# One step of a hybrid decoder layer on one core: gate rows in pieces, x squares on ScalarE, conv and value groups alternating, decode output in column groups

## The chip, the cores and the metric

The kernel runs on one core of one Trainium2 chip. Its engines work side by side, each through its own queue of instructions in order: TensorE (PE; its weight loads are shown as PEld), VectorE (DVE), ScalarE (ACT), GpSimd (POOL) and SyncE (SP, which here only issues DMAs). They wait for each other by semaphores. The metric is the time of the program on the device in microseconds; before the change it is 1457.6 us, the median of three runs (1457.57 to 1459.19).

## The reference

One inference step of a layer for 256 prompt tokens and 8 x 4 decode tokens, width 2048, float32:

```python
h = rms_norm(x, norm_mix); proj = h @ w_in          # 4360 columns: conv q/k, values, output gate, gates, q, k, v
qk = silu(causal_conv(qk_m)); h_m = mlstm_chunkwise(q_m, k_m, v_m, ig, log_sigmoid(fg), C, n, m)
h_m = rms_norm(h_m) * sigmoid(o_m)
a_out = sliding_window_attention(rms_norm(q_a), rms_norm(k_a), v_a, sinks, rel_bias)   # window 128, 16 heads, 2 kv heads
x = x + concat(h_m, a_out) @ w_out
x = x + cross_attend(rms_norm(x), mem_k, mem_v) @ wo    # 4 heads, 256 memory tokens
x = x + square(relu(rms_norm(x) @ w_up)) @ w_down       # 8192 wide
```

The outputs are x and the new states: conv rows, memory matrices C, n and m, window keys and values, memory keys and values.

## The kernel before, in words

Activations lie by feature: 128 features on the partitions, 288 tokens (256 and 32) along the row. All weights come as one stream of 388 chunks, each 512 x 256 numbers (512 KB). SP loads a chunk into one of four slots of `raw`. ScalarE rounds it to the high half `whi` (line 913), VectorE subtracts to get the low half `wlo` (line 1317), and TensorE multiplies high by high, high by low and low by high: 24 matmuls of 128x128 by 288 columns a chunk (line 457). Activations are halved alike (`a_hi`, `a_lo` for x, `b_hi`, `b_lo` for the memory and later for what goes into w_out). Four chunks make a group of 256 output columns, which ends in two of four PSUM tiles `g`; VectorE takes them out.

The first 76 chunks are one written order: groups 0 and 1 memory keys, 2 k and v, 3 to 6 queries (QA), 7 to 10 conv (QKM), 11 to 14 values (VM), 15 to 18 output gate (OM). The table `beside` says for every chunk which smaller steps each engine issues behind that chunk, and every engine goes through the same table: its own part of the chunk (ScalarE and VectorE split the chunk three ahead), then its parts of the steps, then, after a group's fourth chunk, VectorE's taking out. A step that waits on one engine therefore holds all that is queued behind it on that engine, splits and chunk matmuls too.

The steps that the change touches:
- x norm. GpSimd squares the 16 tiles of x and adds them into `nacc` (lines 1976 to 1989); `norm_x` (chunk 11) sums over the partitions with a matmul by ones, ScalarE takes the root, VectorE the reciprocal `rstd`.
- Gate rows. `gates_mm` (11) multiplies x by the gate weights; `gates_rows` (13) is one chain between VectorE and ScalarE (lines 1376 to 1437 and 968 to 978): pre-activations, Exp, Ln, two scans, two more Exp. `columns` (15) turns the rows.
- `mem_squares` (14) and `mem_norm` (18): the norm of the memory rows and keys, squares on ScalarE. `q_norm(n)` (14, 16, 17, 20, 21, 24, 25, 28, 29): square on ScalarE, matmul by a block of ones, root, reciprocal and product.
- Decode attention: `dec_scores` (30), `dec_probs` (32), `dec_out` (33). `dec_out` multiplies by 64 value columns as weights and 32 columns of probabilities as data, 32 matmuls into one bank (lines 569 to 580).
- Sliding window: eight turns of two heads, three chunks apart from chunk 33: `swa_scores` (VectorE adds the bias and takes the maximum), `swa_exp` (ScalarE, with sums), `swa_norm` (VectorE scales the probabilities), `swa_probs` (TensorE turns them, ScalarE and VectorE copy), `swa_out` one chunk on.
- `conv_taps(ct)` for the eight conv tiles at chunks 32 to 45, four multiply-adds on VectorE each; `conv_gate` for all eight at chunk 47 with Sigmoid; `v_turn`, two value tiles each at 50, 53, 56 and 60.
- Memory heads: four heads of four chunks from 60 on: `m_scores`, `m_out0`, `m_out1`, `m_state`, then `m_norm`, `m_gate`, `m_final`. In `m_norm` ScalarE loads the Sqrt table, takes the root, applies Sigmoid to the output gate, and loads Exp again.
- w_out: four turns of two column groups, each group its four chunks in the order of input tiles 8, 12, 0, 4 (`WOUT_KT`); tiles 0 to 7 come from the memory heads.
- Cross-attention (`cross`, one list for all engines) with the value chunks `mv` between, then wo, and `up`/`down` of the MLP, where `rms_total(1)` after the second chunk needs GpSimd's sum of squares.

Of the kernel before, what the change touches and what calls it, by code (L numbers as in the profile page):

```python
# [29 lines left out]
P = 128  # L30
D = 2048
# [38 lines left out]
C_END = 930  # L70
# [15 lines left out]
def constants():  # L86
# [15 lines left out]

    return c
# [26 lines left out]
def weight_stream(w):  # L130
# [7 lines left out]
    for first, groups in ((COL_QA, 4), (COL_QK, 4), (COL_V, 4), (COL_O, 4)):  # L138
        out += tiles(w["w_in"][0], every, range(first, first + groups * CW, CW))
    out += tiles(w["w_out"][0], [r * P for r in WOUT_KT], range(0, D, CW))  # L140
# [34 lines left out]
def gate_columns(w_in):  # L175
# [15 lines left out]
state_in stored memscr_out qz_zero qz_ready dz_hi dz_lo sw_exp sw_max swa_cache swa_new_out tile0_done tile_out u_hi u_lo v_T v_out  # L191
# [3 lines left out]
SLOT_SIGNALS = dict(raw_ready=4, c_in=3, c_out=3, bt_in=2, rb_in=2, vdec_in=2, mv_in=4, mem_in=4, x_in=4, mtok_in=2)  # L195
# [3 lines left out]
    pe_once=dict(xss_bc=1, gates_pre=1, gcols_T=1, kv_T=1, kv_rev=1, dsc_mm=1, dprob_T=1, dout_mm=1, km_T=1, xd_mm=1,  # L199
                 xdp_T=1, xdv_mm=2, xdo_T=1),  # L200
    act_once=dict(rstd_root=1, g_ln=1, gate_rows=1, rm_root=1, ktok_out=2, krev_out=1, kss_root=2, d_exp=1, dpw_out=1,
                  da_hi=4, km_out=2, xd_exp=1, xdp_out=2, od_act=1),
    dve_once=dict(eps_ready=1, wg_split=3, rstd_x=1, g_nz=1, g_exps=1, rm_ready=1, gcols_out=4, kdup_out=2, vtok_out=2,
                  vrev_out=1, memk_ready=8, qd_ready=4, d_max=1, dprob=1, dpn_out=1, da_lo=4, vm_ones=2, xd_max=1,
# [3 lines left out]
def layer_kernel(nc, ins, outs, consts):  # L208
    with ExitStack() as ctx:
# [78 lines left out]
        kgain = view(15328, XHD)  # L288
# [31 lines left out]
        pc, pcT = view(16000, 2, NMEM), view(16512, 2, NMEM)  # L320
# [6 lines left out]
        EPSC, TINY, SSM, RM, KSS, MX, NM, SD, ES, SM = 0, 1, 4, 6, 8, 16, 20, 24, 28, 32  # L327
        GC, WS, WM, NC_, KINV, RM2, SPARE = 36, 48, 60, 68, 104, 112, 114
# [21 lines left out]
        def _(sp):  # L350
# [16 lines left out]
            for j in range(2):  # L367
                load(memtok[:, j, :], ins["mem_prompt"][0, j * P:(j + 1) * P, :], sem["mtok_in"][j])
            with sp.Fori(2, CHUNKS // RING) as i:
# [16 lines left out]
        def dec_src(kv, par):  # L386
            return M[2][kv * HD:(kv + 1) * HD, 0:256].rearrange(
                "p (b t r l) -> p t b r l", b=DB, t=4, r=2)[:, :, :, par, :]
# [17 lines left out]

        def v_bank(i):
# [8 lines left out]
        beside[8].append(("gate_weights",))  # L416
# [14 lines left out]
        for ct in range(8):  # L431
            beside[4 * QKM + 4 + ct % 2 + 4 * (ct // 2)].append(("conv_taps", ct))
        for ct in range(8):
            beside[47].append(("conv_gate", ct))
        for g, c in enumerate((50, 53, 56, 60)):
            beside[c] += [("v_turn", 2 * g), ("v_turn", 2 * g + 1)]
        for h in range(MH):
            for c, what in ((60, "m_scores"), (61, "m_out0"), (62, "m_out1"), (63, "m_state")):
                beside[c + 4 * h].append((what, h))
            if h:  # L440
# [9 lines left out]
                 ("mv", 5), ("xo", 1), ("xs", 3), ("mv", 6), ("xp", 2), ("xm", 3), ("mv", 7), ("xo", 2), ("dv", 0),  # L450
                 ("dv", 1), ("xp", 3), ("dz",), ("xo", 3)]
# [3 lines left out]
        def _(pe):  # L455
# [28 lines left out]
            def norm_x():  # L484

                pe.wait_ge(sem["cst_in"], 16)
                pe.wait_ge(sem["sq_sum"], 16)
                mm(M[0][:, 0:NT], ones, nacc[:, :]).then_inc(sem["pe_once"], 1)
# [1698 lines left out]
```

## Time and profile before

| what | us |
|---|---|
| runs, median of three | 1457.6 |
| profiled execution, its own time | 1460.68 |
| its span, first to last instruction | 1458.9 |
| TensorE busy | 1383.3 |
| VectorE busy | 876.0 |
| ScalarE busy | 606.3 |
| GpSimd busy | 151.4 |

A row of a timeline gives the start in us from the span's start, the duration, engine, line, operation, output and inputs, shape and count; in square brackets stands the idle time of the engine before it and who ended it. "m" and "g" are the PSUM tiles of small steps and of chunks, "arena" is the working memory of most small steps.

### The profile page before, as it was taken

Reading aid. Unit: us, or ns where it says so; the run is one execution under the profiler, and the core shown is the slowest. Engines: PE = TensorE matmul, PEld = TensorE weight load, DVE = VectorE, ACT = ScalarE, POOL = GpSimd, SP = SyncE. Lnnn points to the kernel's source line nnn. Section 1 sums busy time; section 2 is a strip of 40 time slices with the busy share of each in tenths; the row PEclk is TensorE's granted clock in tenths of the full one; section 3 lists DMA queues with packets and bytes.
Section 4 is the critical chain, followed back from the end, with each engine's and each line's share of the span. In section 5 each row is a group of like instructions: output and inputs, shape, how many; then the busy total and the mean of one; then the engine's idle time right before and its main releaser. Section 6 shows DMA issues by size and latency. Waiting matters only on the chain.

```text
span 1458.9 us, 27482 instructions
## 1 busy us (share of the span) xinstructions
PE 1383.3 (95%) x10270; PEld 1349.9 (93%) x10270; DVE 876.0 (60%) x1257; ACT 606.3 (42%) x839; POOL 151.4 (10%) x199
## 2 busy tenths in 40 slices
PE   6749998899999999889999999999999999999999
PEld 6749897888889998789999999999999999999999
DVE  7767698746666667595554455544466544556543
ACT  6445355634454444453333334333343333344332
POOL 4521000011113231260000000000000000000000
PEclk9989999999899999999999999999999999999999
DMA  9754334454538568445554545555454555555553
GB/s 363 237 149 145 116 109 124 126 195 151 160 102 351 169 210 262 149 145 172 160 171 161 164 153 173 173 161 171 158 161 156 179 166 162 169 160 164 166 169 126
DMA packets 74972, 250.06 MB, mean 171 GB/s; under 512 B 8284, under 2 KB 17324, under 8 KB 74512
## 3 DMA queue, kind: packets, MB, share of 16 engines
q1 hardware_dynamic: 58176, 212.36, 44.3%
q0 software_dynamic: 16016, 36.06, 7.9%
q8 instruction: 39, 0.64, 0.2%
q10 hardware_dynamic: 720, 0.83, 0.2%
q14 instruction: 21, 0.17, 0.0%
HBM read 236.20 MB, written 13.64 MB: 171 GB/s over the span
## 4 chain that ended last, share of the span: by engine, by line
PE 80%; DVE 9%; issue 3%; ACT 3%; POOL 2%; DMA 1%; SPq 0%; DVEq 0%; ACTq 0%; POOLq 0%
PE g L457 74%; PE m L457 6%; DVE arena L1303 3%; ACT arena L895 2%; POOL nacc L1983 1%; DVE wlo L1317 1%; DVE arena L1300 1%; DMA raw<-in_stream 1%; POOL nsq L1981 1%; DVE a_lo L1303 1%; ACT whi L913 1%; DVE arena L1292 0%; DVE arena L1296 0%; DVE arena L1306 0%; DVE small L1550 0%
## 5 line engine op out<-in xcount | busy, mean ns | idle before, releaser
L1317 DVE TENSOR_TENSOR wlo<-raw,whi 128x1024 fp32r<-128x1024 f32 x388 | 480.1, 1247 | 375.0 <-ACT whi L913 362.7
L913 ACT ACTIVATE whi<-raw 128x1024 fp32r<-128x1024 f32 x388 | 408.0, 1058 | 472.1 <-PE g L457 440.6
L457 PE MATMUL g<-a_hi,whi 128*128 128x288 f32 x1632 | 362.2, 304 | 8.5 <-issue 5.5
L457 PE MATMUL g<-a_hi,wlo 128*128 128x288 f32 x1632 | 354.7, 299 | 0.0
L457 PE MATMUL g<-a_lo,whi 128*128 128x288 f32 x1632 | 353.6, 298 | 0.0
L457 PE MATMUL g<-b_hi,whi 128*128 128x288 f32 x1344 | 287.9, 295 | 3.8 <-DVE arena L1300 2.7
L457 PE MATMUL g<-b_hi,wlo 128*128 128x288 f32 x1344 | 289.0, 296 | 0.0
L457 PE MATMUL g<-b_lo,whi 128*128 128x288 f32 x1344 | 287.0, 295 | 0.0
L457 PEld LDWEIGHTS g<-a_hi,whi 128*128 128x128 f32 x1632 | 268.1, 192 | 15.8 <-issue 11.7
L457 PEld LDWEIGHTS g<-a_lo,whi 128*128 128x128 f32 x1632 | 267.2, 191 | 0.0
L457 PEld LDWEIGHTS g<-a_hi,wlo 128*128 128x128 f32 x1632 | 266.6, 191 | 0.0
L457 PEld LDWEIGHTS g<-b_hi,whi 128*128 128x128 f32 x1344 | 216.8, 188 | 5.2 <-DVE wlo L1317 3.3
L457 PEld LDWEIGHTS g<-b_lo,whi 128*128 128x128 f32 x1344 | 216.0, 188 | 0.0
L457 PEld LDWEIGHTS g<-b_hi,wlo 128*128 128x128 f32 x1344 | 215.7, 188 | 0.0
L457 PE MATMUL m<-arena 128*128 128x4 f32 (+13 forms) x664 | 84.1, 315 | 17.1 <-DVE arena L1292 10.0
L457 PEld LDWEIGHTS m<-arena 128*128 128x128 f32 (+6 forms) x664 | 65.5, 164 | 32.2 <-issue 17.5
L1300 DVE TENSOR_TENSOR arena<-arena,g 128x288 f32 (+1 forms) x96 | 43.5, 453 | 53.4 <-PE g L457 42.5
L895 ACT ACTIVATE b_hi<-arena 128x288 f32 (+1 forms) x72 | 32.0, 444 | 101.8 <-DVE arena L1303 99.9
L1983 POOL TENSOR_TENSOR nacc<-nacc,nsq 128x288 f32<-128x288 f32 x47 | 50.6, 1076 | 3.7
L1303 DVE SCALAR_TENSOR_TENSOR a_lo<-arena,gcol,a_hi 128x288 fp32r<-128x288 f32 (+1 forms) x48 | 40.7, 848 | 7.3 <-ACT a_hi L895 4.6
L1981 POOL TENSOR_TENSOR nsq<-arena 128x288 f32<-128x288 f32 (+1 forms) x47 | 36.4, 773 | 82.3 <-DVE arena L1300 77.8
L895 ACT ACTIVATE arena<-arena 128x288 f32<-128x288 f32 (+6 forms) x62 | 29.6, 478 | 36.7 <-DVE arena L1303 27.2
(161 smaller groups left out, 767.3 us busy)
## 6 DMA issues: line engine op xcount, KB each, us to landing
raw<-in_stream SPq DMA_DIRECT2D x388, 512.0 KB, 3.4
arena<-in_state_C POOLq DMA_DIRECT2D x8, 512.0 KB, 5.8
out_s_C<-arena POOLq DMA_DIRECT2D x8, 512.0 KB, 4.1
arena<-in_kdT POOLq DMA_DIRECT2D x8, 512.0 KB, 18.1
arena<-in_cache_mem_v POOLq DMA_DIRECT2D x8, 512.0 KB, 8.7
arena<-in_xT SPq DMA_DIRECT2D x4, 576.0 KB, 10.5
arena<-in_xT POOLq DMA_DIRECT2D x1, 2304.0 KB, 9.4
arena<-in_memT SPq DMA_DIRECT2D x4, 512.0 KB, 8.8
```

The source lines that it names most:

```text
L457: return pe.matmul(out, lhsT, rhs, start=start, stop=stop, skip_group_check=True)
L895: return act.activation(out, in_, func, **kw)
L913: act.activation(whi[:, s], raw[:, s], ACT.Copy).then_inc(sem["hi_done"], 1)
L1300: return dve.tensor_tensor(out, a, b, op)
L1303: return dve.scalar_tensor_tensor(out=out, in0=a, scalar=s, in1=b, op0=op0, op1=op1)
L1317: dve.tensor_tensor(wlo[:, s], raw[:, s], f32(whi[:, s]), SUB).then_inc(sem["chunk_split"], 1)
L1981: pool.tensor_tensor(nsq[:, :], x, x, ALU.mult).then_inc(sem["sq_step"], 1)
L1983: pool.tensor_tensor(nacc[:, :], nacc[:, :], nsq[:, :], ALU.add).then_inc(sem["sq_sum"], 1)
```

## The change

- The squares of x are taken by ScalarE from x laid out by tokens: two new loads of 128 x 2048 (`xtok`) and one of the decode tokens in quarters (`xdec`) on SP's queue behind weight chunks 8 and 9; the memory tokens move behind chunks 13 and 14. The sums go onto a diagonal (`diag`), which the matmul by ones spreads over the partitions. GpSimd's 16 squares at the start are gone; its copies of the window caches, which stood behind them, wait for nothing now, and its stores of the memory halves wait for the halves of x.
- `gates_rows` becomes five steps: `gates_a` (chunk 12), `gates_ln` (13), `gates_b` (14), `gates_c` (15), `gates_exp` (16); `columns` moves to 18, the first q_norms to 13, 17 and 18, `mem_squares` to 20, `mem_norm` to 23, `gate_weights` from 8 to 7, the keys' turns one chunk earlier.
- `dec_out` has the probabilities as weights, 32 columns, and 64 value columns as data, four neighbours in four column groups; ScalarE copies the result, and `dec_turn` (35) turns it. It moves to chunk 34.
- Conv and value groups alternate in the weight stream; `conv_taps` come in the value groups, `conv_gate` two chunks behind its taps, `v_turn` at 38, 44, 53 and 60. The value tiles use the conv staging tiles after the taps.
- The scaling of the window probabilities goes from VectorE to four ScalarE activations. Sigmoid becomes (1 + tanh(x/2))/2, with the halves in other factors; in `m_norm` the Exp table is loaded ahead of it and not behind.
- w_out's first turn does input tiles 8 and 12 of both column groups before 0 and 4.
- Cross-attention: two tiles for the turned probabilities in place of one, the fourth head's output in another bank, the copies of the decode output a step of their own (`do`) behind head 2. `rms_total(1)` moves one chunk on.

```diff
-MEMK, KVA, QA, QKM, VM, OM = 0, 2, 3, 7, 11, 15
-WOUT_KT = (8, 12, 0, 4)
+MEMK, KVA, QA, QKM, VM, OM = 0, 2, 3, 7, 8, 15
+W_FIRST = ((0, 8), (0, 12), (1, 8), (1, 12), (0, 0), (0, 4), (1, 0), (1, 4))
+W_NEXT = ((0, 8), (0, 12), (0, 0), (0, 4), (1, 8), (1, 12), (1, 0), (1, 4))
+V_BEFORE = {2: 4, 4: 8, 7: 12}
+V_AFTER = (2, 4, 7)
...
+    for g in range(4):
+        out += tiles(w["w_in"][0], every, (COL_QK + g * CW, COL_V + g * CW))
...
+            for c in range(2 * RING, 4 * RING):
+                chunk(c % RING, ins["stream"][c], c - RING + 1)
+                j = c - 2 * RING
+                if j == 0:
+                    sp.wait_ge(sem["mem_hi"], 16)
+                    sp.wait_ge(sem["mem_lo"], 16)
+                if j < 2:
+                    load(xtok[:, j, :], ins["x_prompt"][0, j * P:(j + 1) * P, :], sem["xtok_in"][j])
+                if j == 1:
+                    load(xdec, ins["x_quarters"], sem["xtok_in"][2])
+                if 5 <= j < 7:
+                    load(memtok[:, j - 5, :], ins["mem_prompt"][0, (j - 5) * P:(j - 4) * P, :], sem["mtok_in"][j - 5])
...
-        for c, what in ((11, "norm_x"), (11, "gates_mm"), (13, "gates_rows"), (14, "mem_squares"), (15, "columns"),
-                        (16, "keys_turn"), (17, "keys_rev"), (18, "mem_norm"), (30, "dec_scores"),
-                        (32, "dec_probs"), (33, "dec_out")):
+        beside[7].append(("gate_weights",))
+        for j in range(3):
+            beside[8 + j].append(("x_squares", j))
+        for c, what in ((11, "norm_x"), (11, "gates_mm"), (12, "gates_a"), (13, "gates_ln"), (14, "gates_b"),
+                        (15, "keys_turn"), (15, "gates_c"), (16, "keys_rev"), (16, "gates_exp"), (18, "columns"),
+                        (20, "mem_squares"), (23, "mem_norm"), (30, "dec_scores"), (32, "dec_probs"), (34, "dec_out"),
+                        (35, "dec_turn")):
             beside[c].append((what,))
-        for n, c in enumerate((14, 16, 17, 20, 21, 24, 25, 28, 29)):
+        for n, c in enumerate((13, 17, 18, 20, 21, 24, 25, 28, 29)):
             beside[c].append(("q_norm", n))
...
         for ct in range(8):
-            beside[4 * QKM + 4 + ct % 2 + 4 * (ct // 2)].append(("conv_taps", ct))
-        for ct in range(8):
-            beside[47].append(("conv_gate", ct))
-        for g, c in enumerate((50, 53, 56, 60)):
+            at = 4 * QKM + 4 + 8 * (ct // 2) + ct % 2
+            beside[at].append(("conv_taps", ct))
+            beside[at + 2].append(("conv_gate", ct))
+        for g, c in enumerate((38, 44, 53, 60)):
             beside[c] += [("v_turn", 2 * g), ("v_turn", 2 * g + 1)]
...
-                            o = M[2][h, b * 32:(b + 1) * 32]
-                            mm(o, vcache[:, b, h], pTw[:, 2 * half + kv, 32 * i:32 * i + 32], True, False)
-                            m = mm(o, vtok[0:32, 2, h], pTn[:, 2 * half + kv, 32 * i:32 * i + 32], False, True)
+                        for i in range(4):
+                            g = slice(32 * i, 32 * i + 32)
+                            mm(M[2][g, at:at + HD], pTw[:, 2 * half + kv, g], vcache[:, 4 * half + i, h], True, False)
+                        for i in range(4):
+                            g = slice(32 * i, 32 * i + 32)
+                            m = mm(M[2][g, at:at + HD], pTn[:, 2 * half + kv, g], vtok[0:32, 2, h], False, True)
...
+            def x_squares(j):                                   # ScalarE
+                act.wait_ge(sem["xtok_in"][j], 16)
+                x = xtok[:, j, :] if j < 2 else xdec
+                A(x, x, ACT.Square, accum_out=sm_(SSX + j)).then_inc(sem["act_once"], 1)
...
+            def swa_norm(t):                                    # ScalarE
+                act.wait_ge(sem["sw_sum"], t + 1)
+                for i in range(4):
+                    v = sc[:, 256 * i:256 * i + 256] if i < 2 else sc[:, 256 + 128 * i:384 + 128 * i]
+                    A(v, v, scale=sm_(SM + i)).then_inc(sem["prob"], 1)
...
-                A(yconv[ct % 2][:, 0:NT], qk[:, ct, :], ACT.Sigmoid).then_inc(sem["conv_sig"], 1)
+                A(yconv[ct % 2][:, 0:NT], qk[:, ct, :], ACT.Tanh, scale=0.5).then_inc(sem["conv_sig"], 1)
...
+            def x_squares(j):                                   # VectorE
+                dve.wait_ge(sem["act_once"], before["x_ssq"] + j + 1)
+                to = slice(P * j, P * j + P) if j < 2 else slice(SEQ, NT)
+                ts(diag[:, to], ident if j < 2 else cst[:, C_SEL:C_END], sm_(SSX + j), MUL).then_inc(sem["dve_once"], 1)
...
-            for kt in range(KT):
-                if kt % CK == 0:
-                    pool.wait_ge(sem["x_in"][kt // CK], 16)
-                add_square(xT[:, kt, :], kt == 0)
```

## Rows read from the trace of the kernel before

**Rows 1.** Page: busy us, share of the span, instructions by engine.

```profile
PE 1383.3 (95%) x10270; PEld 1349.9 (93%) x10270; DVE 876.0 (60%) x1257; ACT 606.3 (42%) x839; POOL 151.4 (10%) x199
```

**Rows 2.** Windows: length, busy (count) PE, PEld, DVE, ACT, POOL; PEclk, DMA share, GB/s.

```profile
11.01:66.07 55.06, 45.89 (x322) 44.82 (x323) 47.98 (x53) 29.85 (x43) 35.53 (x35) 0.94 0.78 288
66.07:112.80 46.73, 28.38 (x200) 26.97 (x199) 27.68 (x55) 22.44 (x35) 13.47 (x25) 0.85 0.64 185
112.80:158.39 45.59, 43.27 (x303) 41.98 (x301) 35.76 (x43) 21.77 (x37) 1.77 (x3) 0.96 0.45 148
158.39:182.93 24.54, 22.53 (x218) 20.02 (x217) 13.93 (x33) 8.17 (x20) 0.00 (x0) 0.87 0.30 93
182.93:310.04 127.11, 116.57 (x868) 110.28 (x867) 103.65 (x237) 71.15 (x153) 7.64 (x11) 0.96 0.40 125
310.04:427.15 117.11, 109.94 (x709) 97.82 (x707) 72.63 (x146) 52.97 (x87) 16.48 (x27) 0.94 0.49 158
...
646.02:1458.90 812.88, 809.78 (x6098) 809.50 (x6096) 424.33 (x509) 293.11 (x316) 0.00 (x0) 1.00 0.51 164
```

**Rows 3.** Timeline of PE, 50 to 60 us.

```profile
56.09 0.82 PE L457 MATMUL g<-a_hi,whi 128*128 128x288 f32 x2 [5.54 <-issue]
```

**Rows 4.** Lines by form, 20 to 47 us: count, busy us, mean ns, idle before.

```profile
L1317 DVE TENSOR_TENSOR wlo<-raw,whi 128x1024 fp32r<-128x1024 f32 x8 | 12.7, 1594 | 0.6 <-ACT whi L913 0.4
...
L1303 DVE SCALAR_TENSOR_TENSOR a_lo<-arena,gcol,a_hi 128x288 fp32r<-128x288 f32 x12 | 11.2, 931 | 0.2
```

**Rows 5.** Lines by form, 110 to 160 us.

```profile
L1317 DVE TENSOR_TENSOR wlo<-raw,whi 128x1024 fp32r<-128x1024 f32 x13 | 15.9, 1225 | 1.4 <-ACT whi L913 1.1
...
L1303 DVE SCALAR_TENSOR_TENSOR arena<-arena,gcol 128x288 f32<-128x288 f32 x7 | 3.6, 518 | 0.2
```

**Rows 6.** DMA issues: count, KB each, median us from issue to landing.

```profile
arena<-in_mem_prompt SPq DMA_DIRECT2D x2, 1024.0 KB, 11.6
...
out_s_swa_k<-in_cache_swa_k POOLq DMA_DIRECT2D x1, 496.0 KB, 2.3
```

**Rows 7.** Lines by form, ScalarE from 66 to 100 us.

```profile
L895 ACT ACT_TABLE_LOAD x3 | 3.8, 1283 | 4.5 <-DVE arena L1300 4.5
L895 ACT ACTIVATE arena<-arena 128x2048 f32<-128x2048 f32 x2 | 3.8, 1901 | 0.0
```

**Rows 8.** Timeline of PE, 66 to 125 us, two waits.

```profile
91.74 1.33 PE L457 MATMUL m<-arena,cst 128*128 128x288 f32 x2 [15.95 <-ACT arena L895]
...
121.77 1.17 PE L457 MATMUL m<-arena,cst 128*128 128x288 f32 x2 [2.32 <-ACT arena L895]
```

**Rows 9.** Timeline of DVE, 113 to 122 us.

```profile
116.55 3.06 DVE L1303 SCALAR_TENSOR_TENSOR arena<-arena,small 128x128 f32<-128x128 f32 x8
```

**Rows 10.** Timeline of PE, 158 to 196 us, small steps.

```profile
159.51 1.14 PE L457 MATMUL m<-arena 64*32 64x128 f32 x64 [1.12 <-DVE arena L1292]
...
172.39 10.60 PE L457 MATMUL m<-arena 128*64 128x32 f32 x72 [0.87 <-DVE arena L1292]
...
195.07 0.93 PE L457 MATMUL m<-arena 64*128 64x256 f32 x8
```

**Rows 11.** Lines by form, 183 to 310 us.

```profile
L457 PE MATMUL m<-arena 128*64 128x128 f32 x96 | 9.9, 296 | 8.0 <-DVE arena L1292 8.0
L895 ACT ACTIVATE arena<-arena,small 128x256 f32<-128x256 f32 x16 | 8.2, 510 | 0.5
...
L895 ACT ACTIVATE arena<-arena,small 128x128 f32<-128x128 f32 x16 | 6.4, 402 | 0.5
...
L1300 DVE TENSOR_TENSOR arena<-arena,small 128x512 f32<-128x512 f32 x8 | 5.5, 692 | 0.3
```

**Rows 12.** Timeline of PE, 250 to 265 us.

```profile
261.12 1.30 PE L457 MATMUL m<-arena 128*64 128x128 f32 x12 [4.36 <-DVE arena L1292]
```

**Rows 13.** Timeline of PE, 596 to 648 us, two waits.

```profile
597.44 1.10 PE L457 MATMUL m<-arena 128*128 128x256 f32 x4 [2.47 <-DVE arena L1296]
...
645.65 0.75 PE L457 MATMUL m<-nacc,cst 128*128 128x288 f32 x2 [1.73 <-POOL nacc L1983]
```

More of the change, by code:

```diff
@@ L137, in weight_stream @@
     out += tiles(w["w_in"][0], every, (COL_KA,))
-    for first, groups in ((COL_QA, 4), (COL_QK, 4), (COL_V, 4), (COL_O, 4)):
-        out += tiles(w["w_in"][0], every, range(first, first + groups * CW, CW))
-    out += tiles(w["w_out"][0], [r * P for r in WOUT_KT], range(0, D, CW))
+    out += tiles(w["w_in"][0], every, range(COL_QA, COL_QA + 4 * CW, CW))
+    for g in range(4):
+        out += tiles(w["w_in"][0], every, (COL_QK + g * CW, COL_V + g * CW))
+    out += tiles(w["w_in"][0], every, range(COL_O, COL_O + 4 * CW, CW))
+    for i in range(4):
+        for g, kt in W_NEXT if i else W_FIRST:
+            out += tiles(w["w_out"][0], (kt * P,), (i * 512 + g * CW,))
     out += tiles(w["wq_x"][0], every, range(0, XW, CW))
@@ L405, in qz_blocks, with xo_bank @@
             return bass.AP(qz.tensor, qz.offset, [list(qz.ap[0]), [DB * ND, XH], [ND + DL, DB], [1, DL]])
+        def xo_bank(h):
+            return M[3 if h < 3 else 2][:, 0:SEQ]
         def v_bank(i):
@@ L724, in _, with w_out @@
             pe.wait_ge(sem["a_lo"], 8)
[L725 to L731 removed]
+            def w_out(i, skip, order):
+                for n, (g, kt) in enumerate(order):
+                    if kt < 8:
+                        pe.wait_ge(sem["m_hi"], kt + CK)
+                        pe.wait_ge(sem["m_lo"], kt + CK)
+                    chunk(4 * WOUT + 8 * skip + n, TL_WOUT + 4 * skip + 2 * g, 1, kt == 8, kt == 4,
+                          more_c=i * 8, more_t=i * 4, kt0=kt)
+            w_out(0, 0, W_FIRST)
+            with pe.Fori(0, 3) as i:
+                w_out(i, 1, W_NEXT)
             def rms_total(n):
[L736 removed]
+                pe.wait_ge(sem["sq_sum"], 16 * (n + 1))
                 mm(M[0][:, 0:NT], ones, nacc[:, :]).then_inc(sem["ss_all"], 1)
@@ L864, in up @@
                           more_c=q * 64 + i * 8, more_t=q * 32 + i * 4, kt0=CK * (n % 4))
-                    if first and n == 1:
+                    if first and n == 2:
                         rms_total(1)
@@ L1026, in dec_out, with dec_turn @@
                 act.wait_ge(sem["pe_once"], before["dout_mm"] + 1)
+                A(dod, M[2][:, 0:256].rearrange("p (a b) -> p a b", a=2)).then_inc(sem["act_once"], 1)
+                act.wait_ge(sem["act_once"], now("dod_out"))
+            def dec_turn():
+                act.wait_ge(sem["pe_once"], before["dout_T"] + 1)
                 act.wait_ge(sem["memscr_out"], 32)
@@ L1250, in up @@
                     split(CH_FFN + 8 * skip + n + RING - 1, q * 64 + i * 8, q * 256 + i * 32)
-                    if first and n == 1:
+                    if first and n == 2:
                         act.wait_ge(sem["ss_all"], 2)
@@ L1793, in _ @@
                             dve.wait_ge(sem["mix_lo"], now("mix_lo"))
+            w_out(0, 0, W_FIRST)
+            with now.loop(3, tile_out=4, mix_lo=4) as i:
+                w_out(i, 1, W_NEXT)
             def ss(h):
@@ L1908, in up @@
                     split(CH_FFN + 8 * skip + n + RING - 1, q * 64 + i * 8)
-                    if first and n == 1:
+                    if first and n == 2:
                         dve.wait_ge(sem["rs_root"], 2)
@@ L2001, in _ @@
             move(rows_scr, rows[:, :], sem["rows_scr_out"])
+            pool.wait_ge(sem["pe_once"], before["gcols_T"] + 1)
+            move(tdec, ins["tdec"], sem["tdec_in"])
             pool.wait_ge(sem["act_once"], before["rm_root"] + 1)
@@ L2004, in _ @@
             move(vcache, ins["cache_swa_v"][0].rearrange("b w k d -> w b (k d)"), sem["swa_cache"])
-            pool.wait_ge(sem["pe_once"], before["gcols_T"] + 1)
-            move(tdec, ins["tdec"], sem["tdec_in"])
             def bias_load(t):
```

264 lines of the change are left out of this document (134 added, 130 removed), and 2 rows, old and new, of the table cross.

## The prediction, made before the changed kernel was run

> **What bounds the kernel now.** I read the page first: TensorE is busy 1383.3 us of 1458.9, 95%, so only about 75 us can be had by waiting less, and a little more where its granted clock drops [rows 1]. Then the stretches: cutting the span where the source changes stage shows that the end of the kernel, 646.02 to 1458.90, is busy 809.78 of 812.88 us; 6098 matmuls there at 24 to a weight chunk make 254 chunks, or 3.20 us a chunk, and the diff moves one wait at its start and nothing else in it [rows 2]. So everything is decided before 646 us, and I price it stretch by stretch as (length minus TensorE busy): 9.2 us idle from 11.01 to 66.07 (A, memory keys, k/v columns and the gates' matmuls), 18.4 to 112.80 (B, gate rows), 2.3 to 158.39 (C, queries), 2.0 to 182.93 (D, decode attention), 10.5 to 310.04 (E, sliding window beside conv and values), 7.2 to 427.15 (M, the memory heads) [rows 2]. The rows of single waits then say who was late.
>
> The sum is made against the profiled execution, 1460.68 us, whose span is 1458.9; it lies 3.1 us above the median 1457.6, and I take 3.1 off at the end.
>
> **A, x norm: -6.3.** The largest wait, 5.54 us before the matmuls at 56.09, is for the last x halves [rows 3]; these and the weight splits are VectorE's, which is busy 47.98 of 55.06 us there [rows 2]. While GpSimd squares x, a split takes 1594 ns and a low half 931 [rows 4]; later, with GpSimd quiet, 1225 and 518 for the same shapes [rows 5]. The change removes GpSimd's squares. Nine splits and sixteen low halves in front of that wait get 9 x 0.37 + 16 x 0.41 = 9.9 us shorter, enough to cover the whole idle time; the granted clock, 0.94 in the mean, gives about 2 more if the wait goes. Against it stand three additions. ScalarE gets two squares of 128x2048 at 1.90 us and one of a quarter: 4.3 us and their accumulator reads [rows 7], 2 of them ahead of the last x tiles. x by tokens (two loads of 1 MB, one of 0.25) goes onto SP's queue behind weight chunks 8 and 9; the memory tokens of the same size leave that place [rows 6], so only 0.25 MB is new there. The two cache copies on GpSimd's queue, 496 KB each, are no longer behind the squares: they start at once, and at the 288 GB/s of this stretch [rows 2] take 3.5 us of the first loads' time. 11.2 less 3.5 less about 1.4 for the square gives 6.3. Bounds: all 11.2 gained; or 3 lost, if copies and squares land in front of the first chunks and the loads, not VectorE, were what VectorE would have met next.
>
> **B, gate rows in pieces: -17.** The 15.95 us before 91.74 end with ScalarE's square for the first key norm [rows 8]. ScalarE got there so late because its order holds the whole gate chain (three table loads of 1.28 us, each answered by VectorE, 4.5 us waited before the last), then both squares of the memory tokens, and only then the key's square [rows 7]. TensorE's order has the key norm in front of chunk 15, so it stands. After, VectorE's first piece is issued one chunk earlier, ScalarE's two logarithm steps stand alone in front of the key norm (two loads and two short activations, about 3.5 us, plus a split, against one chunk of 3.20: some 2 us left), the exponentials come three chunks later (one more load: some 1 us left before the second norm), and the memory squares are gone from here. 18.35 idle becomes 3, and the granted clock of 0.85 [rows 2] means nearly a third of B at 1.2 GHz; most of that was idle, about 2 us were chunk work. 15.3 + 2 = 17. Bounds: 20 with no wait left; 9 if the norm still waits behind half of the chain.
>
> **C, memory rows moved into the queries: +3.** The squares now stand at chunk 20 in front of a query norm of the same chunk: 2 x 1.90 us [rows 7], a root, the query's square and the split before them, some 6 us against one chunk of 3.20: 2.6 us of new wait. The memory key norm moves from chunk 18 to 23. In before, VectorE's eight products of it (3.06 us), a split and two query tiles stood before the query norm two chunks later [rows 9], which waited 2.32 [rows 8]. Now one chunk lies between: 2.32 to 5.5, I take 3.5. Old wait off: 2.6 + 3.5 - 2.3 = 3.8, rounded to 3 as VectorE comes into C less late. Bounds 0 and +6.
>
> **D, decode output: -9.** One group from 172.39 takes 10.60 us: 64 instructions of decode output with 64 columns of weights and 32 of data, and 8 of the first window scores [rows 10]. The 8 alike in the next turn took 0.93 us (x8 at 195.07), so the output is 9.7. In the new form each has 32 columns of weights, four neighbours go to four column groups, and 64 data columns. The row nearest to it is the decode scores, also 32 mm in four column groups: 64 instructions in 1.14 us [rows 10]. I take 1.4 for the output and 0.4 for two transposes: -7.9; and about 1 from the stretch's clock of 0.87 [rows 2]. The added copies on ScalarE lie beside chunks 34 and 35, before the first window probabilities at 36 that need them. Bounds: -10, or 0 if the groups run one after another.
> The rows show the small groups at 1.14 us, with a switch of tile form on each side, and no stall of their own in front of the next chunk. The Trainium skill (TensorEngine Tiling (Array Packing), section Tiling Modes) says that changing the tiling mode drains the engine, which speaks against this edit. By the row D gives 9; by the rule, if the drains were as long as what is saved, it gives the 1 us of the clock alone, which is rival 4.
>
> **E, conv and values alternate, softmax scales on ScalarE: -7.5.** VectorE is busy 103.65 of 127.11 us [rows 2]; the window outputs wait 8.0 us in total for its copies [rows 11], 4.36 of it where all eight conv gates stood at chunk 47 [rows 12]. Per head pair the change takes the scaling of 512 elements (692 ns) and of 256 off VectorE and gives ScalarE four activations of 0.51 and 0.40 [rows 11], 1.8 us. ScalarE, busy 71.15, has room for 8 x 1.8 = 15. Conv taps, which came in four successive groups, now have a value group between them, so VectorE's load is level: its work for three chunks drops under TensorE's. Late next is VectorE itself, whose low half now stands behind ScalarE's scales, some 2 us per turn, mostly covered by three chunks. I leave 3 of 10.5 us idle. Bounds: -12; above, see the last rival.
>
> **The rest.** The memory heads lose one table load of 1.28 us each on ScalarE, beside TensorE work: 0 (bounds -3, +3, as the clock dips there move with activity). The order of w_out removes no wait, as TensorE enters w_out without idling: 0. Cross-attention: 2.47 us before 597.44 waited for the value tiles [rows 13]; probabilities and decode output now fill it: -2.2. The 1.73 us at 645.65 waited for GpSimd's sum [rows 13]; one chunk later it is ready: -1.7.
>
> Sum: -6.3 - 17 + 3 - 9 - 7.5 - 2.2 - 1.7 = -40.7, so 1420.0 in a profiled execution and 1416.9 as a median.
>
> **The rivals.**
> 1. *The front is bound by loads.* For: the DMA share is 0.78 over A [rows 2]. Then removing VectorE's slowdown only shows the landing, A gains nothing: 1423.
> 2. *The stall of B comes back in pieces*, at the key norm, at the memory squares and at the memory key norm, as ScalarE's order is still one queue; 8 more us: 1425. Against it: TensorE has a chunk in front of each piece.
> 3. *The tables.* Tanh does not occur in the trace. If it is loaded apart from Exp, the four pairs of conv gates in E cost two loads each where two stood in all, and each head one more: ten loads of 1.28 us [rows 7], all on the path: 1430. The Trainium skill (ScalarE: Activation LUTs, section Table sets) lists tanh with exp in one set; by that there are none of these, and no run so far shows it.
> 4. *Decode output stays latency bound*: 1425.
> 5. *Slower than before.* Place: E. In every turn ScalarE (exponentials), VectorE (sums), ScalarE (scales), VectorE (low half) now answer each other, and weight splits stand behind both. If the two engines no longer overlap, E lasts 103.65 + 71.15 = 174.8 us for 127.1 [rows 2], and the kernel 1416.9 + 7.5 + 47.7 = 1472. The sign turns when more than 36 of ScalarE's 71 us fall outside VectorE's work. Against it: a turn has three chunks, 9.6 us and more.
>
> **How the numbers follow.** Forecast 0.57; rivals 1 to 5: 0.12, 0.11, 0.07, 0.06, 0.03; better than forecast by several us, 0.04. About 0.2% (3 us) is what can be told from no change. Only rival 5 ends above it; a mixture of two others with a lost clock could end near 1457, 0.02. So faster 0.95, same 0.02, slower 0.03. The bounds of A to E added as independent errors give some 9 us to either side, more above, as rivals 1 to 4 all lie there; two of them together reach 1437: 1405 to 1437.
>
> **What would show it.** A: VectorE's splits before 50 us at 1.22, no wait of 5 us before the eleventh chunk, the gates' matmuls ending near 60. B: the largest wait under 3 us, chunk 18 ending near 89. C: two waits of 2 to 4 us behind the memory rows. D: decode output under 2 us. E: waits of window outputs under 3 us in sum; table loads there two or fewer. It is wrong if B still has a wait near 10, or if E is longer than 127 us.

## The result, and the profile after

The changed kernel takes 1443.4 us (median of four runs, 1443.37 to 1446.03); the kernel before, run beside it, 1458.4. The ratio is 0.9886, 95% interval 0.9859 to 0.9913: faster by about 15 us (1.1%), where 40.7 were predicted. The predicted time, 1416.9 with 1405 to 1437, was too low by 26.5 us and its range did not hold the result. In the profiled executions the span fell by 17.3 us, from 1458.9 to 1441.6, while the sum of the prediction's terms asked for 40.7. The page's line of busy times stands as in [rows 1]:

```profile
PE 1376.8 (96%) x10272; PEld 1344.0 (93%) x10272; DVE 855.9 (59%) x1244; ACT 620.3 (43%) x874; POOL 120.6 (8%) x168
```

VectorE has 20 us less to do, ScalarE 14 more, GpSimd 31 less. The windows, cut where [rows 2] cut the kernel before (A, B, C, D, E, M), say where the time went. Some 3 us of work changed sides of a cut: the decode output (2.4 us) went from D to E, the gate columns and one query norm (some 1 us) from B to C.

```profile
11.22:60.15 48.93, 43.73 (x323) 42.81 (x323) 36.52 (x56) 36.02 (x51) 2.33 (x2) 1.00 1.02 369
60.15:89.88 29.73, 26.14 (x193) 25.06 (x191) 22.15 (x39) 17.50 (x23) 1.70 (x3) 1.00 0.78 206
89.88:140.82 50.94, 44.33 (x309) 42.86 (x308) 41.40 (x59) 28.00 (x50) 13.53 (x24) 0.97 0.55 180
140.82:155.67 14.85, 12.83 (x152) 12.22 (x152) 11.15 (x28) 8.40 (x17) 0.00 (x0) 1.00 0.28 93
155.67:295.68 140.01, 122.33 (x935) 114.37 (x933) 97.30 (x225) 82.42 (x185) 7.65 (x11) 0.93 0.38 118
295.68:413.48 117.80, 110.61 (x709) 98.26 (x707) 72.66 (x146) 49.45 (x84) 16.84 (x27) 0.93 0.50 161
```

| stretch | before | after | difference | predicted |
|---|---|---|---|---|
| A, to chunk 12 | 55.06 | 48.93 | -6.1 | -6.3 |
| B, gate rows | 46.73 | 29.73 | -17.0 | -17 |
| C, queries | 45.59 | 50.94 | +5.4 | +3 |
| D, decode attention | 24.54 | 14.85 | -9.7 | -9 |
| E, sliding window | 127.11 | 140.01 | **+12.9** | **-7.5** |
| M, memory heads | 117.11 | 117.80 | +0.7 | 0 |
| the rest (w_out, cross, MLP) | | | -3.6 | -3.9 |

Five lines came out near their price. E came out on the other side, and its 20.4 us are most of the 23.4 us that are missing (D and E together 19.7, so that the decode output counts in one place). TensorE's timeline after (start, duration, instruction, in brackets the wait before it and who ended it) shows the largest waits of C and E:

```profile
100.13 0.75 PE L486 MATMUL m<-arena,cst 128*128 128x288 f32 x2 [2.75 <-ACT arena L939]
...
117.97 0.75 PE L486 MATMUL m<-arena,cst 128*128 128x288 f32 x2 [3.85 <-ACT arena L939]
...
171.68 1.08 PE L641 MATMUL m<-cst,arena 128*128 128x128 f32 x4 [3.80 <-DVE b_lo L1366]
...
217.22 1.33 PE L667 MATMUL m<-cst,arena 128*128 128x128 f32 x5 [4.38 <-DVE arena L1366]
...
286.62 1.76 PE L486 MATMUL m<-arena 128*64 128x128 f32 x11 [3.14 <-DVE arena L1358]
```

Where [rows 11] and [rows 12] had one kind of late tile (window outputs waiting for VectorE's copies, 8.0 us), E now has several: first window probabilities waiting for the low halves of the decode output, value tiles (217.22) waiting to be taken out, copies again (286.62). All three are VectorE's, as are 16.8 us of all of E's waits together, which are 17.7 us against 10.5. Behind them chunks run at a granted clock under full speed (0.93 in the mean against 0.96): TensorE's busy time in E is 5.8 us longer, 2.4 of it the decode output that moved in.

But VectorE has *less* work there, 97.30 us against 103.65. What it lost shows in its lines by form (count, busy us, mean ns, idle before and who ended it). In the kernel before, 183 to 310 us:

```profile
L1300 DVE TENSOR_TENSOR b_lo<-m,b_hi 128x256 fp32r<-128x256 f32 x8 | 3.4, 424 | 1.9 <-ACT b_hi L895 1.7
```

and in the changed kernel, 156 to 296 us:

```profile
L1366 DVE TENSOR_TENSOR b_lo<-m,b_hi 128x256 fp32r<-128x256 f32 x8 | 3.4, 424 | 17.7 <-ACT b_hi L939 17.7
```

Eight low halves of the window output, 3.4 us of work, have 17.7 us of idle time in front of them. One turn shows why. VectorE's timeline after:

```profile
178.25 1.23 DVE L1383 TENSOR_TENSOR wlo<-raw,whi 128x1024 fp32r<-128x1024 f32 x1
181.04 0.16 DVE L1366 TENSOR_TENSOR small<-small 128x4 f32<-128x4 f32 x1 [1.57 <-ACT small L939]
181.24 0.18 DVE L1372 RECIPROCAL small<-small 128x4 f32<-128x4 f32 x1
183.96 0.42 DVE L1366 TENSOR_TENSOR b_lo<-m,b_hi 128x256 fp32r<-128x256 f32 x1 [2.54 <-ACT b_hi L939]
185.05 1.23 DVE L1383 TENSOR_TENSOR wlo<-raw,whi 128x1024 fp32r<-128x1024 f32 x1 [0.67 <-ACT whi L957]
```

and ScalarE's in the same microseconds:

```profile
180.81 0.20 ACT L939 ACTIVATE small<-small 128x4 f32<-128x4 f32 x1
181.51 1.92 ACT L939 ACTIVATE arena<-arena,small 128x256 f32<-128x256 f32 x4 [0.50 <-DVE small L1372]
183.47 0.39 ACT L939 ACTIVATE b_hi<-m 128x256 fp32r<-128x256 f32 x1
183.89 1.06 ACT L957 ACTIVATE whi<-raw 128x1024 fp32r<-128x1024 f32 x1
```

VectorE gives the reciprocals at 181.42. ScalarE scales for 1.92 us, then takes the high half of the *previous* turn's window output, and only then VectorE may take the low half, the next step in its order. It stands for 2.54 us, seven times so in E, and what is queued behind it (splits, conv, value tiles) starts later by that.

### The profile page after: what moved, and what is told of

Same layout as the page of the kernel before. It is cut to its first block, busy times and chain, and to the rows that moved or that the text cites. A ratio compares the mean times of both kernels' runs of the same rounds, so it can differ in the third digit from the quotient of the medians.

```text
span 1441.6 us, 27415 instructions
## 1 busy us (share of the span) xinstructions
PE 1376.8 (96%) x10272; PEld 1344.0 (93%) x10272; DVE 855.9 (59%) x1244; ACT 620.3 (43%) x874; POOL 120.6 (8%) x168
## 4 chain that ended last, share of the span: by engine, by line
PE 78%; DVE 10%; ACT 6%; issue 4%; DMA 2%; SPq 0%; POOL 0%; DVEq 0%; ACTq 0%
PE g L486 73%; PE m L486 5%; DVE arena L1369 4%; ACT arena L939 3%; DVE wlo L1383 1%; DMA raw<-in_stream 1%; ACT whi L957 1%; DVE arena L1366 1%; DMA arena<-in_memT 1%; DVE arena L1358 1%; DVE a_lo L1369 1%; ACT a_hi L939 1%; DVE arena L1372 0%; ACT b_hi L939 0%; DVE arena L1362 0%
## 5 line engine op out<-in xcount | busy, mean ns | idle before, releaser
L486 PE MATMUL m<-arena 128*128 128x4 f32 (+13 forms) x664 | 77.3, 312 | 13.2 <-DVE arena L1358 7.4
L486 PEld LDWEIGHTS m<-arena 128*128 128x128 f32 (+6 forms) x664 | 59.5, 159 | 28.5 <-issue 13.2
L939 ACT ACTIVATE arena<-arena 128x288 f32<-128x288 f32 (+7 forms) x65 | 34.0, 524 | 31.1 <-DVE arena L1369 23.1
L939 ACT ACTIVATE arena<-m 128x512 f32<-128x512 f32 (+5 forms) x49 | 21.1, 431 | 58.2 <-PE m L486 35.5
L1369 DVE SCALAR_TENSOR_TENSOR arena<-g,rstd 128x288 f32<-128x288 f32 x64 | 29.3, 458 | 23.9 <-PE g L486 22.8
L939 ACT ACTIVATE a_hi<-arena,gcol 128x288 fp32r<-128x288 f32 (+1 forms) x48 | 25.6, 534 | 40.8 <-DVE arena L1366 38.4
## 6 DMA issues: line engine op xcount, KB each, us to landing
arena<-in_xT SPq DMA_DIRECT2D x4, 576.0 KB, 12.3
```

The lines of the kernel that those rows point to most:

```text
L486: return pe.matmul(out, lhsT, rhs, start=start, stop=stop, skip_group_check=True)
L939: return act.activation(out, in_, func, **kw)
L1369: return dve.scalar_tensor_tensor(out=out, in0=a, scalar=s, in1=b, op0=op0, op1=op1)
```

## The experiments

Theory S: the scales, moved to ScalarE, make VectorE wait in its queue. Rival V: the alternating groups load VectorE in bursts, and the scales even helped. Spans are of profiled executions; ratios are against the kernel before on the same chip.

**e1, scales back on VectorE.**

```diff
             def swa_norm(t):                                    # VectorE
-                recip(sm_(SM, 4)).then_inc(sem["sw_sum"], 1)
...
+                softmax_sum()
+                tt(s1, s1, sm_(SM, 2).unsqueeze(2).to_broadcast([P, 2, 256]), MUL).then_inc(sem["dve_step"], 1)
...
+                tt(s0, s0, sm_(SM + 2, 2).unsqueeze(2).to_broadcast([P, 2, P]), MUL).then_inc(sem["prob"], 1)
```

> The changed kernel with one part undone: the scaling of the window probabilities is VectorE's again (two products per turn), ScalarE has no part in it. Theory S (the scales on ScalarE are what made the window stretch long: VectorE's low half of the window output stands behind ScalarE's high half, and that now stands behind four scales; VectorE is idle 17.7 us in front of its low halves against 1.9 before the change): that idle time falls to 3 us or less, VectorE's busy time in the stretch rises by 9, the stretch from the end of chunk 30 to the first memory scores falls from 154.9 us to 142 to 147, and the time from 1443.4 to 1431 to 1436. Rival V (the alternating conv and value groups load VectorE in bursts, and the scales relieved it): VectorE has 9 us more to do in the same bursts, the stretch grows to 158 to 163 and the time to 1447 to 1452.

Measured: span 1426.5 us, ratio 0.9777 (0.9748 to 0.9806). The window of E (length, busy of PE, PEld, DVE, ACT, POOL):

```profile
157.11:281.78 124.67, 115.85 (x934) 109.31 (x933) 105.04 (x239) 68.31 (x153) 7.66 (x11) 0.97 0.42 131
```

The stretch is 15.3 us shorter although VectorE does 7.7 us more in it; from the end of chunk 30 it is 139.5, a little under the expected 142 to 147. The idle time before the low halves is 0.2 us. Rival V is out. Seen from TensorE, 8.9 of the 15.3 us are waits (17.7 to 8.8) and 6.5 are its own work, which ran longer at the lower granted clock (0.93 for 0.97). Another run with the same work in D and E (e7, below) took 139.5 us there too.

**e4, the scales alone, in the kernel before** (the edit of e1 turned round).

> The kernel before with one part of the change alone: the window probabilities are scaled by ScalarE. Theory S: the low halves wait there too, though conv and values do not alternate: the stretch from the end of chunk 30 to the first memory scores grows from 151.7 to 159 to 165 us, the time from 1458.4 to 1466 to 1471. Rival V: VectorE, relieved of 9 us, makes it shorter: 1450 to 1456. If the two nearly cancel (1456 to 1460), the scales hurt only together with the alternation.

Measured: span 1474.8, ratio 1.0097 (1.0065 to 1.0129): slower than before, and by 15.9 us of span, more than the expected 8 to 13; the stretch took 166.96 us where 159 to 165 were expected. Its low halves in E:

```profile
L1307 DVE TENSOR_TENSOR b_lo<-m,b_hi 128x256 fp32r<-128x256 f32 x8 | 3.4, 425 | 19.4 <-ACT b_hi L895 19.4
```

So the loss needs neither the alternating groups nor the new decode output.

**e12, the new decode output alone, in the kernel before** (the diff's `dec_out` and `dec_turn`, at chunks 34 and 35).

> The kernel before with one part of the change alone: decode output with the probabilities as weights in four column groups, at chunk 34, and its turning at 35. The prediction's price for it was 9 us: from the end of chunk 30 to the first memory scores 151.7 becomes 142 to 144, and the time 1449. If its copies and low halves, which now stand in VectorE's and ScalarE's first window turn, cost there (rival): 146 to 148, time 1453. With the run with the scales back (139.5) the rest is what alternating conv and values with the spread gates brings.

Measured: span 1449.3, ratio 0.9944 (0.9923 to 0.9964); from the end of chunk 30 to the first memory scores 145.33 us, between the two expectations. With these, that stretch (D and E together) falls into parts that add up:

| D and E together, us | scales on VectorE | scales on ScalarE | difference |
|---|---|---|---|
| kernel before | 151.65 | 166.96 (e4) | +15.3 |
| with decode output | 145.33 (e12) | | |
| with all of the change | 139.53 (e1) | 154.86 (after) | +15.3 |

Decode output brings 6.3, and the scales on ScalarE cost 15.3 in either order of the work. The 5.8 us from e12 to e1 are what is left over: alternating groups, spread gates and Tanh for Sigmoid, none of them tested alone.

**e2, high half ahead of the scales.** Is it only the order on ScalarE?

```diff
                 beside[34 + 3 * t].append(("swa_out", t - 1))
+            if t < 8:
+                beside[34 + 3 * t].append(("swa_scale", t))
...
-            def swa_norm(t):
+            def swa_scale(t):                                   # ScalarE
```

> The changed kernel with one order turned round: ScalarE does the high half of the window output of the last turn ahead of the four scales of this turn, and VectorE, whose order stays, so gets its low half some 2 us earlier in each of eight turns. Theory S: VectorE's idle time in front of its low halves falls from 17.7 to about 5 us, the stretch from 154.9 to 146 to 150, the time to 1435 to 1439. Rival V: what VectorE saves in waiting it lacks at the next burst of taps; the stretch changes by under 2 us.

Measured: span 1435.6, ratio 0.9829 (0.9801 to 0.9857), E 134.21 us: 5.8 of the 15.3 came back. VectorE's lines in E:

```profile
L1385 DVE TENSOR_TENSOR wlo<-raw,whi 128x1024 fp32r<-128x1024 f32 x28 | 34.3, 1225 | 13.6 <-ACT whi L959 12.9
...
L1371 DVE SCALAR_TENSOR_TENSOR arena<-arena,gcol 128x312 f32<-128x312 f32 x15 | 8.2, 544 | 4.3 <-ACT arena L941 3.9
...
L1371 DVE SCALAR_TENSOR_TENSOR arena<-arena 128x288 f32<-128x288 f32 x8 | 3.7, 457 | 4.8 <-ACT arena L941 4.7
...
L1368 DVE TENSOR_TENSOR b_lo<-m,b_hi 128x256 fp32r<-128x256 f32 x8 | 3.4, 424 | 0.6
```

The wait for the low halves is gone as expected, 17.7 to 0.6, but it has moved down the queue: to the splits (13.6, from 7.3 in the changed kernel), the conv taps (4.3) and the gates (4.8), each of which waits for a ScalarE step that now stands behind the scales. This order does not hide the 1.9 us; no other one was tried.

**e6 and e9, duration or hand-over?** Both leave the scaling out, so they are not the layer any more, but show its time without it. In e6 ScalarE copies four numbers in its place; in e9 TensorE waits for the reciprocal itself.

```diff
-                for i in range(4):
...
-                    A(v, v, scale=sm_(SM + i)).then_inc(sem["prob"], 1)
+                A(sm_(ES, 4), sm_(SM, 4)).then_inc(sem["prob"], 1)
```

> The changed kernel with the scaling of the window probabilities left out (they stay unscaled); in its place ScalarE copies four numbers, so that the hand-over VectorE to ScalarE to TensorE stays, without its 1.9 us. Theory T (the duration of the four scales on ScalarE's queue is what costs): the stretch falls from 140.0 to 118 to 124 and the span from 1441.6 to 1420 to 1426. Theory H (one hand-over more between the two engines in every turn is what costs, whatever it carries): the stretch stays at 134 or more, the span at 1435 or more.

> The changed kernel with the scaling of the window probabilities left out (they stay unscaled) and ScalarE's step too: TensorE waits for VectorE's reciprocal itself. Beside the run without scaling, which still had a hand-over to ScalarE (stretch 125.0 us, span 1431.8). Theory T (only the duration on ScalarE's queue cost): the stretch is within 1.5 us of 125.0. Theory H (the hand-over cost a part of it): it falls to 122 or less.

Measured: e6 span 1431.8, E as in the first fence; e9 span 1418.2, E as in the second.

```profile
156.44:281.42 124.98, 116.95 (x934) 109.89 (x933) 96.19 (x223) 69.77 (x161) 7.66 (x11) 0.97 0.42 131
```

```profile
156.31:275.17 118.86, 115.41 (x935) 108.86 (x934) 96.52 (x223) 68.43 (x153) 7.64 (x11) 0.99 0.44 137
```

Neither theory holds alone. Against none at all, a hand-over with 0.2 us of work costs 6.1 us, 0.8 a turn (4.6 us of it in TensorE's waits, the rest in a lower granted clock); the 1.9 us of real scales cost another 15.0. (In e6 the span exceeds its expectation mostly for other reasons: the memory heads alone took 120.6 us for 117.8, at a lower granted clock; see the last section.) The same scaling on VectorE costs 5.8 us (e1 against e9) for 8.9 us of work.

**e10, half of the scales on ScalarE** (the two narrow pieces; VectorE the wide ones).

```diff
-                for i in range(4):
+                for i in range(2, 4):
...
+                tt(s1, s1, sm_(SM, 2).unsqueeze(2).to_broadcast([P, 2, 256]), MUL).then_inc(sem["sw_wide"], 1)
```

> The changed kernel with the scales shared: VectorE scales the wide half of the probabilities (0.69 us a turn), ScalarE the two narrow pieces (2 x 0.40 us). A dose between none (stretch 125.0) and all four, 1.9 us (140.0). Theory L (there is no slack, every microsecond on ScalarE in this place is one of the turn): 125 + 15 x 0.8 / 1.92 = 131 us, span 1432 to 1434. Rival S (the turn has slack that four scales overrun): 124 to 127 us, span 1425 to 1428.

Measured: span 1433.3, ratio 0.9827 (0.9801 to 0.9854).

```profile
157.87:289.55 131.68, 119.66 (x934) 112.28 (x933) 102.80 (x233) 74.36 (x169) 7.66 (x11) 0.95 0.40 125
```

131.7 us against 131 by theory L: 0, 0.8 and 1.9 us of scales per turn on ScalarE give 125.0, 131.7 and 140.0, close to 8 x 1 us for each. But the middle dose is not a clean one, as VectorE scales the wide pieces in the same microseconds. The low halves in e6 and in e10:

```profile
L1364 DVE TENSOR_TENSOR b_lo<-m,b_hi 128x256 fp32r<-128x256 f32 x8 | 3.4, 424 | 5.7 <-ACT b_hi L939 5.7
```

```profile
L1367 DVE TENSOR_TENSOR b_lo<-m,b_hi 128x256 fp32r<-128x256 f32 x8 | 3.4, 424 | 5.1 <-ACT b_hi L940 5.1
```

VectorE waits no longer than with no scales at all, and has 6.6 us more to do (102.80 against 96.19): its own part accounts for the 6.7 us as well as ScalarE's does. Whether a turn has slack for 0.8 us on ScalarE alone stays open.

**e3, decode output one chunk earlier** (`dec_out` at 33, `dec_turn` at 34).

> The changed kernel with decode output back at chunk 33 and its turning at 34, one chunk earlier each. Theory D (the 3.80 us before the first window probabilities is the decode output's low half, four VectorE products behind ScalarE's scales and the first conv gate): that wait goes, and with it the half-clock chunk behind it: 3 to 5 us less, 1438 to 1440. Rival: the first turn is late by its own chain, and the wait is put down to the window's softmax or to the weight split instead: within 1 us of 1443.

Measured: span 1442.2, ratio 0.9880 (0.9852 to 0.9907): no gain, against my expectation. The 3.80 us fell to 0.21, and came back in pieces: TensorE's waits in the next turns, 1.18 and 0.91 us near 186, and

```profile
207.33 1.11 PE L486 MATMUL m<-arena 128*64 128x128 f32 x12 [2.41 <-DVE arena L1358]
```

for the 1.71 of the changed kernel. Moving this step in VectorE's queue only moved the wait.

**e5, value tiles later** (on e1: the second pair turned at 46 instead of 44).

> Scales on VectorE as in the run with the scales back, and the turning of the second pair of value tiles at chunk 46 instead of 44, so that two chunks more lie between VectorE's taking out of those tiles (behind chunk 43) and the matmuls that turn them. Theory W (the 4.60 us in front of this turning come from its place, one chunk behind its group): they go, with the 1.5 us of the half-clock chunk behind them: the stretch from chunk 34 to the first memory scores falls from 124.7 to 118 to 120, and the span from 1426.5 to 1420 to 1422. Rival: VectorE is the bound of that burst anyway and the wait comes back in front of the next window output or score: under 2 us gained.

Measured: span 1423.6, ratio 0.9789 (0.9773 to 0.9806), E 122.30 from 124.67. Under half of what was expected (118 to 120): the 4.60 us went, and waits of 0.51 and 1.38 us appeared at the window output and at the new place. Its rival names the rest.

**e7, memory rows later** (on e1).

```diff
-                        (20, "mem_squares"), (23, "mem_norm"), ...
+                        (22, "mem_squares"), (26, "mem_norm"), ...
```

> Scales on VectorE, and the squares of the memory tokens at chunk 22 instead of 20, the memory keys' norm at 26 instead of 23: two chunks without a query norm lie behind each. Theory Q (the waits of 2.75 and 3.85 us among the queries come from a query norm in the same chunk or one behind): both go or fall under 2 us in sum, the slow chunk behind the second too, the stretch of the queries falls from 50.9 to 45 to 47 and the span from 1426.5 to 1421 to 1423. Rival: ScalarE and VectorE have the same work and are as late at the next query norm: within 2 us of 1426.5.

Measured: span 1423.3, ratio 0.9793 (0.9765 to 0.9821). C:

```profile
92.51:139.78 47.27, 42.81 (x309) 41.34 (x308) 41.29 (x59) 27.90 (x50) 13.58 (x24) 1.00 0.62 195
```

Shorter by 3.7 us; the waits of 2.75 and 3.85 became 2.14 and 2.32, now behind other work of VectorE. The place was a part of their cause, not all.

**e8, e1 with e5, e7 and e3 together.**

> All together: scales on VectorE, the second value tiles turned at chunk 46, memory rows at 22 and 26, decode output at 33 and its turning at 34. If the steps are independent: 5 from the values, 5 from the memory rows and 2 from the decode output's low half (1.83 us before the first probabilities with the scales back), so a span of 1413 to 1417. If VectorE's work in the first window turns is what sets them (theory from the run with decode output early, where the wait only moved): nothing from the last, 1416 to 1419.

Measured: span 1422.5, ratio 0.9776 (0.9759 to 0.9793), above both expected ranges. D and E together are 137.3 us, as in e5 alone (137.2), C 47.3 as in e7; the early decode output again brings nothing. The memory heads took 118.6 us against 116.9 in e1, which took back some of it.

**e11, the queries once more** (e5 with `columns` and `mem_squares` at 22, `mem_norm` at 26, half of its products at 28).

> Scales on VectorE, second value tiles at chunk 46, and among the queries: the gate columns at 22 instead of 18, the squares of the memory tokens at 22, the memory keys' norm at 26 with half of its eight products put off to 28. Theory Q (the 2.14 us before the query norm at chunk 20 are the gate columns of two chunks before, 2.3 us of VectorE, and the 2.32 before that at 28 the products): both fall under 1 us, the stretch of the queries from 47.2 to 43 to 45, and the span to 1417 to 1420. Rival: VectorE's reciprocals, 1.95 us for each of nine norms, are the bound there, and the stretch stays at 46 to 47.

Measured: span 1420.3, ratio **0.9737** (0.9713 to 0.9762), the best version, 2.6% under the kernel before and about 1.5% under the changed one. The windows of C and of the memory heads:

```profile
92.17:135.91 43.74, 42.79 (x309) 41.37 (x308) 39.68 (x57) 27.95 (x50) 13.54 (x24) 1.00 0.63 196
273.65:392.62 118.97, 111.51 (x709) 99.35 (x707) 73.80 (x148) 49.44 (x84) 16.84 (x27) 0.92 0.50 161
```

C has 1 us of idle time left, under what it had before the change. The decode scores behind it wait 2.67 us instead of 1.11: the put-off products reach into their copies. And with 119.0 us of memory heads, against 116.9 in e1, the span ended just above the expected 1417 to 1420.

## Why the prediction was wrong, step by step

Of the 23.4 us that are missing, the scales on ScalarE are 15.3, the decode output 2.7 (6.3 for 9), the rest of E 1.7 (5.8 for 7.5), C 2.4; what is left is 1.3. The prediction had named its own sign of being wrong, E longer than 127 us, and E took 140; of its smaller signs two were missed, decode output under 2 us (2.04) and window outputs waiting under 3 us in E (5.4).

- **A, right** (-6.1 for -6.3), by the mechanism named: with GpSimd quiet the splits between 20 and 47 us take 1225 ns for 1594 and the low halves 516 for 931, against [rows 4].

```profile
L1383 DVE TENSOR_TENSOR wlo<-raw,whi 128x1024 fp32r<-128x1024 f32 x9 | 11.0, 1225 | 5.7 <-ACT whi L957 5.6
L1369 DVE SCALAR_TENSOR_TENSOR a_lo<-arena,gcol,a_hi 128x288 fp32r<-128x288 f32 x12 | 6.2, 516 | 0.2
```

  The largest wait left is 1.95 us for 5.54; the loads moved 369 GB/s for 288 and did not hold the stretch at its length (rival 1 out). What the loads and the squares took, 3.5 and 1.4 us in the sum, no run separates. The Trainium skill (GPSIMD Engine Reference, section Key points) says that GpSimd shares its SBUF interfaces with VectorE's instructions of two SBUF inputs; the split is one, and the rows agree.
- **B, right** (-17.0 for -17): the waits left in place of the 15.95 of [rows 8] are 2.01, 0.66 and 0.93 us, near the 2 and 1 named. Rival 2 did not come: the new waits among the queries are those that C had priced.
- **C, right in kind, too small** (+5.4 for +3): the waits stood where the prediction put them, 2.75 for 2.6 at the squares and 3.85 for 3.5 at the key norm. What was mis-sized: the waits grew by 4.3 us for the 3.8 summed, the rounding down, "as VectorE comes into C less late", took off 0.8 us that did not go, and 1.1 us of TensorE's work lies in C now (gate columns and a query norm, from across the cut). The granted clock had no part in it: 0.97 for 0.96.
- **D, right in its stretch, too large as a term, and by a mechanism that was in part another**: -9.7 there, but the output's 2.04 us and its turning, 0.38, now lie in E, and alone (e12) the edit brings 6.3. The 64 instructions took 2.04 us for 9.7 before and for the 1.4 taken from the decode scores. Rival 4 is out.

```profile
159.05 2.04 PE L486 MATMUL m<-arena 128*32 128x64 f32 x64
161.02 0.54 PE L486 MATMUL g<-a_hi,whi 128*128 128x288 f32 x2
```

  Four neighbours did start beside each other, within 0.02 us. But the starts of the single instructions in the trace show something else too. The group has two forms, weights on 128 rows (the cache) and on 32 (the new tokens). Wherever one follows the other, 0.14 to 0.15 us lie between the two starts at full clock; within a form it is 0.06 at most in the new order and 0.05 to 0.08 in the old. The old order changed form after every second instruction, 31 times, and these gaps add up to 5.6 of its 9.7 us (0.15 us each, 0.22 at the lower granted clock); the new order changes after every eighth, 7 times, 1.0 of its 2.04 us. So more than half of what the group gained lies at the changes of form, which the prediction did not count. The Trainium skill (TensorEngine Tiling (Array Packing), section Tiling Modes) says that a change of the tiling mode drains the engine; these gaps fit that, but no run separates the drain from anything else.
- **E, the step that failed** (+12.9 for -7.5). The prediction did name the wait: VectorE, "whose low half now stands behind ScalarE's scales, some 2 us per turn", measured 2.5. It then called this "mostly covered by three chunks" and put it at nothing; it cost 15.3 us. That is the error: cover was counted in TensorE's chunks, but the one that stands is VectorE, and what TensorE needs next is queued behind it. E can be laid out as VectorE's busy time, ScalarE's time outside it, and the time in which neither works (worked out by laying the two timelines over each other): before 103.7 + 15.7 + 7.7, after 97.3 + 33.9 + 8.8, e1 105.0 + 12.3 + 7.3, e9 96.5 + 15.5 + 6.9 us. That these add up to E is true by construction; what they show is where the change went: 6 us less of VectorE's work, 18 us more in which VectorE stands while ScalarE works. The argument that ScalarE "has room" was a busy share, which says nothing of when its answer is due. The other half of the term, levelled conv work, was near: 5.8 us by what is left over.
- **Rival 5 was the mechanism, at part strength and at a chance of 0.03.** The same edit alone (e4) made the kernel slower; in the whole change the other terms outweighed it. It was priced only at no overlap at all, 47.7 us; the prediction's own 1.8 us of scales per turn, eight times and all on the path, would have given 14.6, near the 15.3 between e1 and the changed kernel. That is in part luck: against no scaling at all (e9) the scales on ScalarE cost 21.1 us, hand-over and lower clock included. Its sign of a turn was summed wrong: with E as 103.65 us plus ScalarE's time outside VectorE's work, and the rest as forecast, the whole is slower than before from 57 us outside on, not from 36. So the 33.9 measured (36.4 in e4) decide nothing by their nearness to 36.
- **The small ones, right**: M +0.7 for 0; cross-attention -1.9 for -2.2, the sum of squares and the MLP -2.1 for -1.7, w_out +0.4 for 0. Rival 3 is out: E shows no table load among ScalarE's groups, where it had two. The Trainium skill (ScalarE: Activation LUTs, section Table sets) has tanh in one set with exp, and the trace agrees.

## What to carry to other kernels

Before work is moved from a busy engine to an idle one, follow the order of both queues: if the busy engine's next step answers the idle one's, the work moved can come back as a wait, plus the hand-over. Here 1.9 us a turn came back whole, though ScalarE had been busy only 56% of the stretch. Cover counts only on the engine that waits. Which engine bounds a stretch is read from who ends TensorE's waits in it, not from busy shares; and a reordering there can just move the wait (e2, e3). Ask of an order of small matmuls, too, how often the form changes in it.

## What the runs showed of the hardware that was not expected

The hand-over itself: one activation of 128x4, 0.2 us, put between VectorE's reciprocal and TensorE costs 0.8 us a turn. It must wait for VectorE and so holds the high half behind it: VectorE's low halves wait 5.7 us with it (e6) and 0.6 without (e9).

The memory heads' length varies from 114 to 121 us among kernels whose code and waits there are the same (7.0 to 7.5 us of idle TensorE time in all), with the granted clock. The windows of this stretch in e2 and in e6:

```profile
292.20:406.25 114.05, 106.94 (x709) 95.02 (x707) 73.82 (x148) 49.44 (x84) 16.85 (x27) 0.96 0.52 168
```

```profile
281.42:402.03 120.61, 113.11 (x708) 100.85 (x707) 73.79 (x148) 49.45 (x84) 16.88 (x27) 0.91 0.49 158
```

0.96 and 0.91 of full clock, 6.6 us apart: as much as most single edits here were worth. The queries show it once too: 53.6 us in e5 at a granted clock of 0.90, and 50.9 to 51.0 at 0.97 in the changed kernel and five other runs, with the same code and the same 6.6 us of waits there. Comparing stretches, and not only times, kept the two apart. What decides which chunks run slow there was not found.
